# Four stationary buffers of a split-precision encoder block moved to other byte offsets in SBUF

## Chip, core and metric

The kernel runs on one core of a Trainium2 chip. The metric is the device time of one execution in microseconds (us), lower is better. One execution was also taken with the hardware profiler, and the rows below are from that one.

## What is computed

One encoder block on a sequence of 1024 tokens with 1024 features, in float32. Cut to what matters here:

```python
mod = silu(c) @ w_ada + b_ada                      # 6 rows: shift, scale, gate, twice
h = rmsnorm(x, g_norm1) * (1 + sc1) + sh1
z = h @ w_in                                       # 1024x1024 @ 1024x7168: seven groups of 1024 columns
y_a = (b_a * depthwise_conv(c_a * x_a, conv_a)) @ w_a_out
u = depthwise_conv(u_b * sigmoid(v_b), conv_b) + b_conv_b       # 31 taps
y_b = silu(layernorm(u, ln_g, ln_b)) @ w_b_out
x = x + gt1 * ((sigmoid(g_a) * y_a + sigmoid(g_b) * y_b) @ w_o)
h = rmsnorm(x, g_norm2) * (1 + sc2) + sh2
# top-1 of 4 groups, then top-2 of its 8 experts; rows sorted into blocks of 128 of one expert
yb = (silu(xblk @ w_gate[e]) * (xblk @ w_up[e])) @ w_down[e]
x = x + gt2 * scatter(w * yb)
out = rmsnorm(x, g_final)
```

## The kernel before

**Split products.** Every large matrix is kept as two float32r parts: `hi`, the value cast to float32r, and `lo`, what is left of it. The helper `three` issues three matmuls for each product of a 128x128 stationary tile and a 128x512 moving tile: hi by hi (line 1688), hi by lo (line 1689) and lo by hi (line 1690). Each matmul comes with its own weight load (LDWEIGHTS), also where two in a row have the same stationary tile. In the profile a matmul is written `ps<-moving,stationary`, so `ps<-A_hi,w_hi` has the weights `w_hi` as its stationary operand and `A_hi` as its moving one.

**Stages, in order of time.**
1. Set-up, until about 68 us: modulation rows, norm, transposes of the input.
2. The input projection: 56 slabs of weights (8 channel groups of 7 kinds), then 8 slabs of `w_a_out` and 8 of `w_b_out`, until about 840 us. A slab is 1024x128 weights. It is loaded into one of three slots of `w_raw`, ScalarE casts it to `w_hi` (line 816), VectorE writes `w_lo = w_raw - w_hi` (line 1097), and TensorE runs 48 matmuls with slices `w_hi[:, slot, k*128:(k+1)*128]` and the same of `w_lo` as stationary operand. The moving operand is `A_hi`/`A_lo`, for `w_b_out` `B_hi`/`B_lo`. Meanwhile VectorE does the two depthwise convolutions (line 1260 makes most of the 31 taps of the longer one).
3. The output projection `w_o`, until about 950 us: stationary `A_hi`/`A_lo`, moving `B_hi`/`B_lo`. Router and block tables follow until about 1000 us. The router matmul (line 1909) has the stationary operand `s2`, for the last tile `x1T_last`.
4. The experts, until about 1560 us: 33 blocks, in a loop that is unrolled four times. Each block has 48 matmuls with stationary `xT_hi`/`xT_lo` (gate and up, moving `e_hi`/`e_lo`) and 24 with stationary `hT_hi`/`hT_lo` (down). ScalarE casts each expert chunk to `e_hi` (lines 963, 969), VectorE makes `e_lo` (lines 1552, 1556). In front of these stand eight transposes of the token rows (line 2013) and, in the middle of gate and up, four of the hidden rows (line 2018).
5. The last blocks, the final norm and the stores.

All engines run the code in the order in which it is written, with semaphores between them.

**Places in SBUF.** All buffers are put by hand with `at(name, offset, ...)`, which adds a base address. `T4` is 4096 bytes. `oA`, `oAl`, `oB`, `oBl`, `oW`, `oS`, `oR` and `oM` are the offsets of regions, each before the change a multiple of 4096, and later stages use the same bytes under other names. `oX`, the expert stage's region for `xT_hi` and `xT_lo`, is a multiple of 4096 too. In this text the place of a buffer is its offset from the base modulo 512. The moving slices of the split products step by 2048 or 4096 bytes and the stationary ones by 512, so that each buffer's place is also that of each of its slices. Before the change it is 0 for every stationary and every moving buffer of `three`. Some operands of other matmuls lie elsewhere: `ident`, `ones`, `mean_w` and `s2` at 128, `same_token` at 256.

Of the kernel before, what the change touches and what calls it, by code (L numbers as in the profile page):

```python
# [26 lines left out]
F32 = mybir.dt.float32  # L27
F32R = mybir.dt.float32r
# [5 lines left out]
P = 128  # L34
# [38 lines left out]
def encoder_block(nc, x, c, w_ada, b_ada, g_norm1, w_in, conv_a, w_a_out, conv_b, b_conv_b, ln_g, ln_b,  # L73
                  w_b_out, w_o, g_norm2, w_rg, b_rg, w_re, b_re, w_gate, w_up, w_down, g_final, out):
    S, D = x.shape
    KT = D // P
# [8 lines left out]
    FT = F // P  # L85
# [7 lines left out]
    with ExitStack() as ctx:  # L93
# [3 lines left out]
        def at(name, offset, shape, dtype):  # L97
            return nc.alloc_sbuf_tensor_at(name, shape, dtype, offset=base + offset)

        T4 = 4 * D  # L100
        oA, oAl, oB, oBl = 0, 8 * T4, 16 * T4, 24 * T4
        oW = 32 * T4
        oS = oW + 9 * T4
        oR = oS + 4 * T4
        oM = oR + 4 * T4

        A_hi = at("A_hi", oA, [P, KT, S], F32R)
        A_lo = at("A_lo", oAl, [P, KT, S], F32R)
# [20 lines left out]
        conv_acc_b = at("conv_acc_b", oBl + 4 * T4 + 32, [P, S], F32)  # L129
        gate_st = at("gate_st", oBl + 5 * T4 + 32, [P, 2, S], F32)  # L130
        w_raw = at("w_raw", oW, [P, 3, KT * P], F32)
        w_hi = at("w_hi", oW + 3 * T4, [P, 3, KT * P], F32R)
        w_lo = at("w_lo", oW + 6 * T4, [P, 3, KT * P], F32R)
        wo_buf = [at(f"wo_raw{i}", oW + o * T4, [P, D], F32) for i, o in enumerate((4, 7, 5, 8))]
        stream = at("stream", oS, [P, 4, D], F32)
        rows = at("rows", oR, [P, 4, D], F32)
        GT1, SH2, A2, GT2 = range(4)
# [93 lines left out]
        s_last = at("s_last", oM + 2624, [P, 1], I32)  # L231
        act_warm = at("act_warm", oM + 2656, [P, 1], F32)
        hT_hi = at("hT_hi", oM + 4096, [P, FT, P], F32R)
        hT_lo = at("hT_lo", oM + 4096 + 2048, [P, FT, P], F32R)


        NCH = 6
# [1902 lines left out]
```

## Time and profile before

| | |
|---|---|
| time, median of 3 runs | 1593.94 us (1591.94 to 1595.24) |
| time of the profiled execution | 1591.27 us |
| its span, first to last instruction | 1589.6 us |
| TensorE (PE) busy | 1551.8 us, 98% |
| VectorE (DVE) busy | 1317.7 us, 83% |
| ScalarE (ACT) busy | 677.8 us, 43% |
| GpSimd (POOL) busy | 356.1 us, 22% |
| mean granted TensorE clock | 0.992 |

The span is shorter than the execution by 1.67 us, which lies around it. Matmuls are pipelined: the duration of one runs from its start until its result has drained, and the next one starts before that. So the rate of TensorE is read from the distance between the starts of two matmuls, which is called the pitch here, and not from their duration. PEld is the weight load, which has rows of its own.

### The profile page before, as it was taken

The numbers are of one execution on the slowest core, as the hardware profiler recorded it, in microseconds if no ns is written. First come the engines' busy times: TensorE is split into PE (matmuls) and PEld (weight loads), VectorE is DVE, ScalarE is ACT, GpSimd is POOL, SyncE is SP. The second block draws the span as 40 slices with busy tenths as digits, with TensorE's granted clock in tenths as the row PEclk, the third lists the DMA queues.
The fourth block names the chain that finished last, engine by engine and source line by source line (L and its number), as shares of the span: only waits on it lengthen the run. The fifth ranks groups of instructions, "written<-read, shape, count | busy, mean of one in ns | idle before, by whom it ended". The sixth has DMA issues, their size and how long they took to land.

```text
span 1589.6 us, 21208 instructions
## 1 busy us (share of the span) xinstructions
PE 1551.8 (98%) x7106; PEld 1272.9 (80%) x7106; DVE 1317.7 (83%) x1127; ACT 677.8 (43%) x574; POOL 356.1 (22%) x225
## 2 busy tenths in 40 slices
PE   8999999999999999999999999999999999999994
PEld 4788888888888888878888887788888888888882
DVE  5696969797978787798447469999999999999996
ACT  6511111111111010334223126777777777777764
POOL 2000000000001010000001003354455445554541
PEclk9999999999999999999999999999999999999997
DMA  9241323232323241744554347999999999999976
GB/s 358 97 120 67 119 90 108 92 117 68 119 66 119 66 124 49 238 139 133 176 174 152 119 151 292 399 371 398 398 371 376 385 379 393 376 392 392 378 274 240
DMA packets 167951, 352.61 MB, mean 222 GB/s; under 512 B 17479, under 2 KB 91239, under 8 KB 167907
## 3 DMA queue, kind: packets, MB, share of 16 engines
q1 hardware_dynamic: 150836, 309.57, 53.1%
q0 software_dynamic: 16992, 42.32, 8.8%
q8 instruction: 25, 0.41, 0.1%
q10 hardware_dynamic: 81, 0.17, 0.0%
q14 instruction: 17, 0.14, 0.0%
HBM read 324.90 MB, written 46.67 MB: 234 GB/s over the span
## 4 chain that ended last, share of the span: by engine, by line
PE 88%; DVE 5%; DMA 3%; issue 2%; ACT 1%; SPq 0%; DVEq 0%; POOLq 0%; POOL 0%; ACTq 0%
PE ps L1688 28%; PE ps L1690 28%; PE ps L1689 28%; PE ps L2013 2%; DMA xn<-in_x_dram 1%; PE ps L2018 1%; DMA w_raw<-in_w_in_dram 1%; DVE e_lo L1552 1%; PE ps L1909 1%; PE ps L1823 1%; DVE f_o L1652 0%; DVE s L1332 0%; PE ps L1893 0%; DMA e_raw<-in_w_up_dram 0%; DMA e_raw<-in_w_down_dram 0%
## 5 line engine op out<-in xcount | busy, mean ns | idle before, releaser
L1688 PE MATMUL ps<-A_hi,w_hi 128*128 128x512 f32 x1024 | 400.0, 391 | 2.3 <-DVE A_lo L1180 1.8
L1690 PE MATMUL ps<-A_hi,w_lo 128*128 128x512 f32 x1024 | 398.4, 389 | 0.0
L1689 PE MATMUL ps<-A_lo,w_hi 128*128 128x512 f32 x1024 | 398.4, 389 | 0.0
L1260 DVE SCALAR_TENSOR_TENSOR conv_acc_b<-glu,colc,conv_acc_b 128x1024 f32<-128x1024 f32 x232 | 298.0, 1285 | 10.2 <-DVE rows L1243 0.6
L1552 DVE TENSOR_TENSOR e_lo<-e_raw,e_hi 128x2048 fp32r<-128x2048 f32 x132 | 300.7, 2286 | 4.1 <-ACT e_hi L963 3.6
L963 ACT CAST e_hi<-e_raw 128x2048 fp32r<-128x2048 f32 x132 | 252.2, 1913 | 44.7 <-PE ps L1690 36.0
L1688 PEld LDWEIGHTS ps<-A_hi,w_hi 128*128 128x128 f32 x1024 | 192.2, 188 | 44.8 <-issue 3.9
L1689 PEld LDWEIGHTS ps<-A_lo,w_hi 128*128 128x128 f32 x1024 | 192.2, 188 | 40.4 <-issue 0.7
L1690 PEld LDWEIGHTS ps<-A_hi,w_lo 128*128 128x128 f32 x1024 | 192.2, 188 | 40.0
L1688 PE MATMUL ps<-e_hi,xT_hi 128*128 128x512 f32 x528 | 212.2, 402 | 0.0
L1690 PE MATMUL ps<-e_hi,xT_lo 128*128 128x512 f32 x528 | 206.4, 391 | 0.0
L1689 PE MATMUL ps<-e_lo,xT_hi 128*128 128x512 f32 x528 | 205.7, 390 | 0.0
L1556 DVE TENSOR_TENSOR e_lo<-e_raw,e_hi 128x2048 fp32r<-128x2048 f32 x64 | 146.0, 2283 | 0.0
L700 POOL DMA_INDIRECT d_x<-y_sb,s_idx x31 | 85.9, 2771 | 252.1 <-DVE y_sb L1577 228.0
L816 ACT CAST w_hi<-w_raw 128x1024 fp32r<-128x1024 f32 x72 | 73.7, 1046 | 156.5 <-PE ps L1690 153.4
L1097 DVE TENSOR_TENSOR w_lo<-w_raw,w_hi 128x1024 fp32r<-128x1024 f32 x72 | 88.0, 1223 | 60.9 <-ACT w_hi L816 57.7
L969 ACT CAST e_hi<-e_raw 128x2048 fp32r<-128x2048 f32 x64 | 122.4, 1915 | 37.5 <-PE ps L1690 37.5
L1690 PEld LDWEIGHTS ps<-e_hi,xT_lo 128*128 128x128 f32 x528 | 99.1, 188 | 21.9
L1688 PEld LDWEIGHTS ps<-e_hi,xT_hi 128*128 128x128 f32 x528 | 99.6, 189 | 18.9 <-DVE e_lo L1552 0.2
L1689 PEld LDWEIGHTS ps<-e_lo,xT_hi 128*128 128x128 f32 x528 | 99.4, 188 | 18.8
L696 POOL DMA_INDIRECT xg<-d_h,g_idx x33 | 101.2, 3067 | 28.3 <-POOL g_idx L694 28.3
L1688 PE MATMUL ps<-e_hi,hT_hi 128*128 128x512 f32 x264 | 103.0, 390 | 3.6 <-DVE hT_lo L1571 3.6
(329 smaller groups left out, 2028.5 us busy)
## 6 DMA issues: line engine op xcount, KB each, us to landing
e_raw<-in_w_gate_dram SPq DMA_DIRECT2D x132, 512.0 KB, 5.6
e_raw<-in_w_up_dram SPq DMA_DIRECT2D x132, 512.0 KB, 7.1
e_raw<-in_w_down_dram SPq DMA_DIRECT2D x66, 1024.0 KB, 7.8
w_raw<-in_w_in_dram SPq DMA_DIRECT2D x56, 512.0 KB, 4.3
stream<-in_w_ada_dram SPq DMA_DIRECT2D x36, 512.0 KB, 6.0
xn<-in_x_dram SPq DMA_DIRECT2D x8, 512.0 KB, 11.1
ada_a<-in_w_ada_dram SPq DMA_DIRECT2D x8, 512.0 KB, 10.1
d_short<-conv_acc_a POOLq DMA_DIRECT2D x8, 512.0 KB, 4.0
```

The costliest lines, as they stand in the source:

```text
L696: g.indirect_dma_start(xg[:, slot, :], None, d_h2, bass.IndirectOffsetOnAxis(ap=g_idx[:, slot:slot + 1], axis=0), bounds_check=S - 1, oob_ ...
L700: g.indirect_dma_start(d_x1, bass.IndirectOffsetOnAxis(ap=idx_ap, axis=0), rows_ap, None, bounds_check=S - 1, oob_is_err=False, compute_op ...
L816: a.copy(w_hi[:, slot, :], w_raw[:, slot, :]).then_inc(w_hi_done, 1)
L963: a.copy(e_hi[:, q, :], e_raw[:, q, :]).then_inc(gu_hi, 1)
L969: a.copy(e_hi[:, 4 + q, :], e_raw[:, 4 + q, :]).then_inc(d_hi, 1)
L1097: v.tensor_tensor(w_lo[:, slot, :], w_raw[:, slot, :], w_hi[:, slot, :].bitcast(F32), ALU.subtract).then_inc(w_lo_done, 1)
L1260: lstep(v.scalar_tensor_tensor(conv_acc_b[:], glu[:, t:t + S], w, conv_acc_b[:], ALU.mult, ALU.add))
L1552: v.tensor_tensor(e_lo[:, q, :], e_raw[:, q, :], e_hi[:, q, :].bitcast(F32), ALU.subtract).then_inc(gu_lo, 1)
L1556: v.tensor_tensor(e_lo[:, 4 + q, :], e_raw[:, 4 + q, :], e_hi[:, 4 + q, :].bitcast(F32), ALU.subtract).then_inc(d_lo, 1)
L1688: t.matmul(dst, st_hi, mv_hi, start=first, stop=False)
L1689: t.matmul(dst, st_hi, mv_lo, start=False, stop=False)
L1690: return t.matmul(dst, st_lo, mv_hi, start=False, stop=last)
```

## The change

Nothing but addresses: no instruction, operand shape, order or semaphore is touched, and the instruction lists of all five engines are the same as before, row for row.

```diff
-        oS = oW + 9 * T4
+        oS = oW + 9 * T4 + 256
         oR = oS + 4 * T4
-        oM = oR + 4 * T4
+        oM = oR + 4 * T4 + 32
...
-        w_hi = at("w_hi", oW + 3 * T4, [P, 3, KT * P], F32R)
-        w_lo = at("w_lo", oW + 6 * T4, [P, 3, KT * P], F32R)
-        wo_buf = [at(f"wo_raw{i}", oW + o * T4, [P, D], F32) for i, o in enumerate((4, 7, 5, 8))]
+        w_hi = at("w_hi", oW + 3 * T4 + 64, [P, 3, KT * P], F32R)
+        w_lo = at("w_lo", oW + 6 * T4 + 256, [P, 3, KT * P], F32R)
+        wo_buf = [at(f"wo_raw{i}", oW + o * T4 + shift, [P, D], F32) for i, (o, shift) in enumerate(((4, 64), (7, 256), (5, 64), (8, 256)))]
...
-        hT_lo = at("hT_lo", oM + 4096 + 2048, [P, FT, P], F32R)
+        hT_lo = at("hT_lo", oM + 4096 + 2176, [P, FT, P], F32R)
```

`w_hi` goes to place 64, `w_lo` to 256, `hT_hi` to 288 and `hT_lo` to 416. The stationary buffers `A_hi`, `A_lo`, `xT_hi` and `xT_lo` stay at 0, as do all moving operands of `three`. With `oS`, `stream` and `rows` move by 256 bytes. With `oM`, everything behind it moves by 288: `glu`, `s2`, `ident`, `ones`, `mean_w`, the small columns and the tables of the expert stage. `wo_buf`, four buffers for raw rows of `w_o`, lies in slots of `w_hi` and `w_lo` and goes with them. All moves are multiples of 32 bytes.

## Rows read from the trace of the kernel before

**Rows 1.** The profile page: busy share, and the granted clock in 40 slices

```profile
PE 1551.8 (98%) x7106; PEld 1272.9 (80%) x7106; DVE 1317.7 (83%) x1127; ACT 677.8 (43%) x574; POOL 356.1 (22%) x225
...
PEclk9999999999999999999999999999999999999997
```

**Rows 2.** The page's chain that ended last, by engine

```profile
PE 88%; DVE 5%; DMA 3%; issue 2%; ACT 1%; SPq 0%; DVEq 0%; POOLq 0%; POOL 0%; ACTq 0%
```

**Rows 3.** Windows (from:to, length, busy us and count): projections, experts, one block

```profile
68.00:840.00 772.00, 771.68 (x3382) 634.27 (x3382) 602.25 (x482) 152.74 (x153) 36.53 (x40) 1.00 0.36 114
...
1000.00:1550.00 550.00, 550.00 (x2593) 459.15 (x2593) 542.49 (x341) 409.02 (x275) 277.62 (x125) 1.00 1.00 377
...
1100.80:1118.60 17.80, 17.80 (x86) 14.87 (x85) 17.77 (x12) 13.37 (x9) 9.19 (x5) 1.00 1.03 404
```

**Rows 4.** Groups by line and form on PE: count, busy us, mean ns

```profile
L1688 PE MATMUL ps<-A_hi,w_hi 128*128 128x512 f32 x1024 | 400.0, 391 | 2.3 <-DVE A_lo L1180 1.8 <-DVE A_lo L1189 0.3 <-DVE w_lo L1097 0.2
...
L1688 PE MATMUL ps<-e_hi,xT_hi 128*128 128x512 f32 x528 | 212.2, 402 | 0.0
...
L1688 PE MATMUL ps<-e_hi,hT_hi 128*128 128x512 f32 x264 | 103.0, 390 | 3.6 <-DVE hT_lo L1571 3.6
...
L1688 PE MATMUL ps<-B_hi,A_hi 128*128 128x512 f32 x128 | 50.3, 393 | 0.0
L1688 PE MATMUL ps<-B_hi,w_hi 128*128 128x512 f32 x128 | 50.0, 391 | 0.3 <-DVE w_lo L1097 0.3
```

**Rows 5.** Timeline (start us, us) in the projection: nineteenth after first, and one pair

```profile
726.71 0.39 PE L1688 MATMUL ps<-A_hi,w_hi 128*128 128x512 f32 x1
...
730.79 0.39 PE L1688 MATMUL ps<-A_hi,w_hi 128*128 128x512 f32 x1
...
300.17 0.39 PE L1688 MATMUL ps<-A_hi,w_hi 128*128 128x512 f32 x1
300.17 0.19 PEld L1689 LDWEIGHTS ps<-A_lo,w_hi 128*128 128x128 f32 x1
```

**Rows 6.** Timeline of PE just behind the four transposes of a block

```profile
1101.43 0.40 PE L1689 MATMUL ps<-e_lo,xT_hi 128*128 128x512 f32 x1
...
1101.90 0.40 PE L1688 MATMUL ps<-e_hi,xT_hi 128*128 128x512 f32 x1
...
1103.75 0.39 PE L1690 MATMUL ps<-e_hi,xT_lo 128*128 128x512 f32 x1
```

**Rows 7.** Timeline of PE, matmuls of plain float32 and the router's

```profile
18.81 0.59 PE L1719 MATMUL ps<-ada_a,diag_c 128*128 128x512 f32 x1
...
20.12 1.88 PE L1719 MATMUL ps<-ada_a,diag_c 128*128 128x512 f32 x4
...
679.65 1.88 PE L1817 MATMUL ps<-conf_sum,mean_w 128*128 128x512 f32 x4
...
873.66 1.40 PE L1909 MATMUL ps<-w_r,s 128*128 128x36 f32 x11
...
947.80 1.40 PE L1909 MATMUL ps<-w_r,x1T_last 128*128 128x36 f32 x11
...
1566.18 1.88 PE L2110 MATMUL ps<-y_prev,same_token 128*128 128x512 f32 x4
```

**Rows 8.** One line's durations: the taps on DVE, min/median/max ns

```profile
L1260 DVE SCALAR_TENSOR_TENSOR conv_acc_b<-glu,colc,conv_acc_b x232: 1277/1285/1290, 71.4 to 684.0; 128x1024 f32<-128x1024 f32 x116
```

**Rows 9.** The page's groups of the two that write the weight parts

```profile
L816 ACT CAST w_hi<-w_raw 128x1024 fp32r<-128x1024 f32 x72 | 73.7, 1046 | 156.5 <-PE ps L1690 153.4
L1097 DVE TENSOR_TENSOR w_lo<-w_raw,w_hi 128x1024 fp32r<-128x1024 f32 x72 | 88.0, 1223 | 60.9 <-ACT w_hi L816 57.7
```

**Rows 10.** The page's DMA issues: the only large loads whose target moves

```profile
stream<-in_w_ada_dram SPq DMA_DIRECT2D x36, 512.0 KB, 6.0
```

## Prediction

> **What bounds the kernel.** I read the page first: TensorE is busy 98% of the span, at the full granted clock until the last slice [rows 1], and the chain that ended last runs over TensorE for 88% of it [rows 2]. The windows by stage say the same of each stage: 771.68 of 772 us in the two projections, where VectorE has 602, and 550 of 550 us among the experts, where VectorE has 542.5 and the DMA engines are busy all the time [rows 3]. The groups show that TensorE hardly waits: 2.3 us before all first matmuls of the projection, 3.6 us before those of the down product [rows 4]. So a change that moves no instruction can do something only if it changes what one matmul costs, and then almost every nanosecond counts.
>
> What one costs is the pitch. From the first to the nineteenth start of the projection rows are 4.08 us for 18 matmuls, 226.7 ns each, and the load of the next weights starts together with each matmul [rows 5]. The reader is to see that the duration of 389 to 391 ns [rows 4] is no cost; the pitch is.
>
> **The change part by part.** It removes, adds and orders nothing. Three kinds of operand move.
>
> *Stationary reads of TensorE.* With `w_hi` and `w_lo` as stationary operand there are three times 1024 matmuls of A and three times 128 of B, 3456 in all; with `hT_hi` and `hT_lo` three times 264, which is 792 [rows 4]. Together 4248. One nanosecond of pitch is 3.46 us in the projections and 0.79 us among the experts. The price per matmul is not shown by the trace, since all operands of `three` lie at place 0, so I bound it.
>
> From above in time: directly behind the transposes the same instructions, with the same places, run slower. The first two steps take 0.47 us, 235 ns each, and the first ten 2.32 us, 232 ns each, before the pitch falls to its steady value [rows 6]. So the pitch isn't a constant of the instruction: how weight load and moving stream fall against each other has a price of 5.3 ns (mean) to 8.3 ns (worst). If a new place held them in such a relation for good, that would be 4248 x 5.3 = 22.5 us to 4248 x 8.3 = 35.3 us.
>
> From below: a plain float32 matmul of 512 columns has a pitch of (1.88 - 0.59) / 3 = 430 ns, and a weight load of its own each time [rows 7]. If it streams its columns twice, one stream takes 215 ns beside a weight load, an estimate from these rows. The split matmul streams once and takes 226.7. The 11.7 ns between may be what the weight load takes from the moving stream when that runs at full rate. If another place took all of it away, the projections would win 3456 x 11.7 = 40.4 us. Among the experts it would be 792 x 11.7 = 9.3 us, but VectorE leaves no more than 550 - 542.5 = 7.5 us there [rows 3]. The lower bound is therefore -47.9 us.
>
> Which value between? I take 0, for three reasons from rows. First, where stationary operands at different places can be compared they cost the same: `diag_c` at 0, `mean_w` at 128 and `same_token` at 256 all give 1.88 us for four, and the router's weight loads from `s2` at 128 and from `x1T_last` at 0 both give 1.40 us for eleven, at most 127 ns each, though their moving operand has 36 columns and the load of 128 columns is the longer part [rows 7]. A weight load by itself doesn't care where it reads. Second, a load reads one run of exactly 512 bytes, and a moving stream beside it reads four such runs. [...] Third, 226.7 ns holds for operands that lie far apart in different ways (A with w, B with w, B with A, e with hT, means of 389 to 393 ns in all of them [rows 4]). None of this tests a full-rate stream at another place, so the chance stays well under certainty.
>
> [...]
>
> *VectorE and ScalarE.* VectorE writes `w_lo` 72 times and reads `w_hi`, `rows`, `stream`, `glu` and `hT_hi` at new places. The 232 taps of line 1260 read `glu` from starts that lie 4 bytes apart, and all take 1277 to 1290 ns [rows 8]. So place costs VectorE at most those 13 ns, and for the 72 + 31 + 33 instructions on `w_lo`, `y_sb` and `hT_lo` that is 1.8 us of engine time. The part in the projections lies under TensorE, since VectorE has 170 us to spare there [rows 3]; without that cover the 72 would cost 0.9 us. The cast to `w_hi` has 153 us of waiting for TensorE ahead of it [rows 9]. In the expert block VectorE is busy 17.77 of 17.80 us [rows 3], so the rest, 64 x 13 ns = 0.8 us, is the most that could show. I take 0.
>
> *DMA.* `w_raw` and the expert chunks don't move. Only `stream`'s target does, by 256 bytes, in 512 KB loads that take 6.0 us [rows 10] in a stage where the DMA engines are 36% busy [rows 3]. I take 0. If a load took 10% longer it would land 0.6 us later, and what it feeds would have to be waited for to show.
>
> **Sum.** 1591.27 + 0 + 0 + 0 = 1591.3 us for a profiled execution. That one lay 2.7 us under the median of the runs shown, so for the median I add it again: 1593.9 us. What a measurement of this kernel can tell from no change is about 0.2%, 3.2 us here, or 0.75 ns on each of the 4248 matmuls. A dependence on place that is there at all would most likely be larger than that, so the cases stand apart.
>
> **The rivals.**
> 1. *The place frees the moving stream.* For it: the 11.7 ns that no wait explains, equal places of weights and moving operand, and the fact that they start in the same instant [rows 5], so that they begin on the same spot of every 512 bytes. Against it: the three reasons above. At full effect 1593.9 - 40.4 = 1553.5 us, with what VectorE lets through among the experts down to 1546.0. Since the four buffers have four places, a part is as likely as the whole: with half the effect, or with only `w_hi` helped in part, 1574. [...]
> 2. *The place fixes a worse relation.* One mechanism: each matmul keeps the pitch that now lasts only ten matmuls behind a transposition [rows 6], because load and stream no longer start on the same spot. It is decided by whether 226.7 ns is the settled best or merely the value for place 0. Price 22.5 us, 1616.4 us in all; with only one of the stationary pair affected about half, 1605; at worst 1629.2. It turns from no change to slower at 0.75 ns per matmul. Among the experts nothing absorbs it, as TensorE has no idle time there. Against it: the pitch always falls back to 226.7 by itself, and does so in all pairings.
> 3. *The places cancel.* `w_hi` serves two of three matmuls and `w_lo` one. A gain on one and a loss on the other would end near zero with both pitches changed. It is counted in the forecast's chance, and a small part of it in the others.
>
> **How the numbers follow.** No change within 0.2%: 0.56. Rival 1: 0.24, since the unexplained 11.7 ns needs some cause. Rival 2: 0.20. The likeliest case's own range is 1590.7 to 1597.1 us. To hold 8 in 10 the range must take in 0.24 of the others. I put half of rival 1 at a gain of 24 us or less, which reaches to 1570, and rather more than half of rival 2 at a loss of 12 us or less, to 1606. What stays outside is 0.12 and 0.08.
>
> **What would show it.** In the profile of the changed kernel, the pitch of `ps<-A_hi,w_hi` to `ps<-A_lo,w_hi` and of `ps<-A_hi,w_lo` should be 227 ns as before; `ps<-e_hi,xT_hi` and `ps<-B_hi,A_hi`, whose stationary buffers stay, are the control in any case. The projection window should still hold some 3382 matmuls in 772 us, and the expert block 17.80 us. Rival 1 would show a pitch toward 215 ns on `w_hi` or `w_lo` rows alone and a projection stage of 732 us, while the block would shrink by a few tenths at most. Rival 2 would show 230 to 235 ns in both. A different stage length at an unchanged pitch would mean that I missed a wait, and a block longer than 17.80 us at an unchanged pitch would put it on VectorE. The prediction is wrong if a full-rate moving stream and a weight load do disturb each other by where they lie, which nothing in the trace of before could try.

## The result and the profile after

The changed kernel takes 1614.85 us (median of 4 runs, 1610.91 to 1617.51) against 1592.94 us for the kernel before on the same occasions: a ratio of 1.0137, 95% interval 1.0123 to 1.0152. It is slower by about 22 us, outside the range of 1570 to 1606, and close to the 1616.4 us of rival 2.

The page of the changed kernel, its busy row and its chain, show a longer span and no new wait of TensorE:

```profile
PE 1580.3 (98%) x7106; PEld 1274.5 (79%) x7106; DVE 1317.8 (82%) x1127; ACT 677.0 (42%) x574; POOL 305.3 (19%) x225
...
PE 91%; DVE 3%; DMA 3%; issue 1%; ACT 0%; SPq 0%; DVEq 0%; POOLq 0%; POOL 0%; ACTq 0%
```

Against [rows 1] VectorE has the same 1317.8 us of work, ScalarE too, and TensorE 28.5 us more. The windows of the same stretches as in [rows 3] show where it is:

```profile
68.00:840.00 772.00, 772.00 (x3293) 617.05 (x3292) 588.33 (x470) 144.30 (x144) 36.52 (x40) 1.00 0.34 108
1000.00:1550.00 550.00, 547.47 (x2571) 453.86 (x2570) 541.83 (x340) 411.80 (x279) 224.05 (x122) 1.00 1.02 383
1124.00:1141.90 17.90, 17.90 (x85) 14.87 (x84) 17.70 (x13) 13.37 (x9) 9.29 (x6) 1.00 1.03 403
```

In the same 772 us TensorE is as busy and gets through 3293 matmuls, not 3382. The granted clock of that window is 1.00 in both kernels, and 0.992 in the mean of both executions, so it is not the clock. (The 547.47 busy us in the window from 1000 us are no new wait: everything there stands 22 us later, so that the window now takes in the first waits of the expert stage. From 1022.3 us on TensorE is busy for 527.68 of 527.70 us.) The groups by form (count, busy us, mean ns) say which ones take longer:

```profile
L1688 PE MATMUL ps<-A_hi,w_hi 128*128 128x512 f32 x1024 | 405.9, 396 | 0.3 <-DVE A_lo L1189 0.3
...
L1688 PE MATMUL ps<-e_hi,xT_hi 128*128 128x512 f32 x528 | 211.2, 400 | 0.0
...
L1688 PE MATMUL ps<-e_hi,hT_hi 128*128 128x512 f32 x264 | 104.9, 397 | 3.3 <-DVE hT_lo L1571 3.3
```

A mean of 396 for `w_hi` stands against 391 in [rows 4] and 397 for `hT_hi` against 390, while `xT_hi`, whose place stayed, has 400 and 402. The timeline gives the pitch. These are the first and the eighth `A_hi,w_hi` of a stretch. Each of them is followed by its `A_lo,w_hi` and `A_hi,w_lo`, so the two rows are 21 matmuls apart:

```profile
299.63 0.40 PE L1688 MATMUL ps<-A_hi,w_hi 128*128 128x512 f32 x1
...
304.52 0.39 PE L1688 MATMUL ps<-A_hi,w_hi 128*128 128x512 f32 x1
```

4.89 us for 21 is 233 ns, against 226.7 in [rows 5]. The sum closes. With A as moving operand the 3072 matmuls run from 43.6 to 751.2 us before and from 45.0 to 772.1 us after (starts of `A_hi,w_hi`), 707.6 and 727.0 us, which is 19.4 us or 6.3 ns each. With B it is 753.0 to 839.8 before and 773.2 to 862.3 after (starts of `B_hi,w_lo`), 2.3 us more. The down products lie between 999.8 and 1563.8 us before and 1022.3 and 1590.1 us after (starts of `e_hi,hT_hi`), 3.8 us more; the distance from block to block grew from 17.80 to 17.92 us. Together 25.5 us, where the two spans differ by 26.3 us. The first projection also began 1.4 us later in this execution, and 0.7 us came back between the last `A_hi,w_hi` and the first `B_hi,w_lo` (1.8 us before, 1.1 after). This execution was the slowest of the four of the changed kernel; the medians differ by 21.9 us.

### The profile page after: what moved, and what is told of

Same layout as the page of the kernel before. It is cut to its first block, busy times and chain, and to the rows that moved or that the text cites. A ratio compares the mean times of both kernels' runs of the same rounds, so it can differ in the third digit from the quotient of the medians.

```text
span 1615.9 us, 21208 instructions
## 1 busy us (share of the span) xinstructions
PE 1580.3 (98%) x7106; PEld 1274.5 (79%) x7106; DVE 1317.8 (82%) x1127; ACT 677.0 (42%) x574; POOL 305.3 (19%) x225
## 4 chain that ended last, share of the span: by engine, by line
PE 91%; DVE 3%; DMA 3%; issue 1%; ACT 0%; SPq 0%; DVEq 0%; POOLq 0%; POOL 0%; ACTq 0%
PE ps L1690 29%; PE ps L1688 29%; PE ps L1689 29%; PE ps L2013 2%; DMA xn<-in_x_dram 1%; PE ps L2018 1%; DMA stream<-in_w_ada_dram 1%; PE ps L1909 1%; DVE e_lo L1552 1%; PE ps L1823 1%; DVE f_o L1652 0%; PE ps L1893 0%; DVE e_lo L1556 0%; DMA e_raw<-in_w_down_dram 0%; PE ps L1817 0%
## 5 line engine op out<-in xcount | busy, mean ns | idle before, releaser
L1688 PE MATMUL ps<-A_hi,w_hi 128*128 128x512 f32 x1024 | 405.9, 396 | 0.3 <-DVE A_lo L1189 0.3
L1690 PE MATMUL ps<-A_hi,w_lo 128*128 128x512 f32 x1024 | 405.3, 396 | 0.0
L1689 PE MATMUL ps<-A_lo,w_hi 128*128 128x512 f32 x1024 | 403.3, 394 | 0.0
L1689 PE MATMUL ps<-e_lo,hT_hi 128*128 128x512 f32 x264 | 103.8, 393 | 0.0
## 6 DMA issues: line engine op xcount, KB each, us to landing
xn<-in_x_dram SPq DMA_DIRECT2D x8, 512.0 KB, 11.1
```

The costliest lines, as they stand in the source:

```text
L1688: t.matmul(dst, st_hi, mv_hi, start=first, stop=False)
L1689: t.matmul(dst, st_hi, mv_lo, start=False, stop=False)
L1690: return t.matmul(dst, st_lo, mv_hi, start=False, stop=last)
```

## Experiments

### 1. The pattern by itself, at 28 combinations of places

A kernel with nothing but the split matmuls. `hi` and `lo` are the places of the stationary pair, `m` is that of the moving operand. The code is shortened, and the line of the moving slices is put in words (in bytes); the slices of `st` are in elements of 4 bytes:

```python
for r in range(2):
    for k in range(8):
        for h in range(2):
            m_hi, m_lo = moving slices at (k % 4) * 4096 + h * 2048 + m, two buffers
            s_hi, s_lo = st[:, hi + k * P:hi + (k + 1) * P], st[:, lo + k * P:lo + (k + 1) * P]
            t.matmul(dst, s_hi, m_hi, start=k == 0, stop=False)
            t.matmul(dst, s_hi, m_lo, start=False, stop=False)
            t.matmul(dst, s_lo, m_hi, start=False, stop=k == 7)
```

> This kernel leaves the block's computation out: it runs nothing but the split matmul pattern (hi by hi, hi by lo, lo by hi, 128x512, a weight load each) 96 times in each of 28 sections, with eight plain float32 matmuls between sections. Section by section the places of the stationary pair and of the moving operand differ: 16 sections with hi and lo at the same place 0, 32, ... 480 and the moving operand at 0; six with unequal pairs, those of the change among them; six with the moving operand at 64 or 256 too, and two places below 32 bytes. Theory A, the distance between stationary and moving place sets the pitch: it goes up and down over the 16 sections by some ns around 227, 64/64/64 and 256/256/256 have the 226.7 ns of 0/0/0. Theory B, the stationary buffer's own place does: 64/64/64 is as slow as 64/64/0. Theory C, only an unequal pair is slow, because each load finds another relation than the one before: all 16 equal sections have 226.7 ns and 64/256/0 and 288/416/0 have 231 to 234 ns.

Like all sweeps here, this is one profiled execution. The steady pitch, worked out from the starts of the matmuls behind the 24th of each section:

| place of hi and lo, moving operand at 0 | ns |
|---|---|
| 0 and 256 | 226.7, 226.7 |
| 32 and 288 | 233.3, 233.3 |
| 64 and 320 | 233.2, 233.2 |
| 96 and 352 | 234.3, 234.3 |
| 128 and 384 | 232.3, 232.3 |
| 160 and 416 | 233.3, 233.3 |
| 192 and 448 | 228.9, 228.9 |
| 224 and 480 | 233.3, 233.3 |

Places 256 apart are one place. Of the other sections, 4 and 16 have 232.4 and 233.3 ns, the pair (0, 64) has 231.1, (64, 0) has 233.3, and (0, 256), (256, 0) and place 0 with the moving operand at 256 have 226.7. The same can be read straight from the timeline, at the starts of the plain matmuls that stand between sections. The distance of two such rows is one section of 96 split matmuls with the plain ones next to it:

```profile
173.29 0.49 PE L67 MATMUL ps<-raw 128*128 128x128 f32 x3
197.06 0.49 PE L67 MATMUL ps<-raw 128*128 128x128 f32 x3
221.25 0.49 PE L67 MATMUL ps<-raw 128*128 128x128 f32 x3
244.84 0.49 PE L67 MATMUL ps<-raw 128*128 128x128 f32 x3
...
556.96 0.49 PE L67 MATMUL ps<-raw 128*128 128x128 f32 x3
580.54 0.49 PE L67 MATMUL ps<-raw 128*128 128x128 f32 x3
604.12 0.49 PE L67 MATMUL ps<-raw 128*128 128x128 f32 x3
627.90 0.49 PE L67 MATMUL ps<-raw 128*128 128x128 f32 x3
```

The first four enclose the sections 192, 224 and 256: 23.77, 24.19 and 23.59 us. The last four enclose 64 and 256 with the moving operand at the same place, both 23.58 us, as fast as 0, and then stationary 0 with the moving operand at 64: 23.78 us, which is the value of 192, that is of -64. So theory A holds: what counts is the distance from the moving operand, modulo 256 bytes. B falls. C falls too, since equal pairs are slow at seven of eight places. The pairs of the change gave 231.1 ns, both (64, 256) and (288, 416).

### 2. The parts of the change, and the distance, in the kernel

Diffs of kernels are against the changed kernel, unless the text says otherwise. They are cut to the buffers that matter; `wo_buf` goes with the slots that it lies in each time. First, only hT and the small buffers stay moved:

```diff
-        w_hi = at("w_hi", oW + 3 * T4 + 64, [P, 3, KT * P], F32R)
-        w_lo = at("w_lo", oW + 6 * T4 + 256, [P, 3, KT * P], F32R)
+        w_hi = at("w_hi", oW + 3 * T4, [P, 3, KT * P], F32R)
+        w_lo = at("w_lo", oW + 6 * T4, [P, 3, KT * P], F32R)
```

> The changed kernel with w_hi, w_lo and the raw rows of w_o back at place 0, so that only hT_hi (288) and hT_lo (416) and the small buffers stay moved. If the loss is the sum of 3456 matmuls with w and 792 with hT at some 6 ns each, the projections are back at their old length and the time is 1594 + 4 = 1598 us, with an expert block of 17.92 us. If the loss came from a moved small buffer or from stream and rows, it stays near 1615 us.

1595.51 us, ratio 1.0022 (1.0011 to 1.0034), a block distance of 17.92 us and 226.7 ns with w. The ratio stands for 3.5 us, the medians differ by 2.6. In the profile the down products span 3.9 us more than before and the projections are back to within 1 us. So that is the experts' part, and the small buffers, `stream` and `rows` cost nothing that can be seen.

Both of a pair at one place:

```diff
-        w_lo = at("w_lo", oW + 6 * T4 + 256, [P, 3, KT * P], F32R)
+        w_lo = at("w_lo", oW + 6 * T4 + 64, [P, 3, KT * P], F32R)
...
-        hT_lo = at("hT_lo", oM + 4096 + 2176, [P, FT, P], F32R)
+        hT_lo = at("hT_lo", oM + 4096 + 2048, [P, FT, P], F32R)
```

> The changed kernel with hi and lo of each pair at one place: w_hi and w_lo at 64, hT_hi and hT_lo at 288. Theory C (only unequal pairs are slow) gives the time of before, 1593 us. Theories A and B (the place itself) give 233 ns on the matmuls with w if 64 is a bad place, 1610 to 1617 us, or anything down to 1593 us if it is 256 that is bad.

1619.23 us, ratio 1.0170 (1.0153 to 1.0186), slower than the change itself, with a block of 17.97 us. Its timeline, 21 matmuls from the first row to the second:

```profile
299.85 0.39 PE L1688 MATMUL ps<-A_hi,w_hi 128*128 128x512 f32 x1
...
304.75 0.39 PE L1688 MATMUL ps<-A_hi,w_hi 128*128 128x512 f32 x1
```

4.90 us, 233.3 ns. Theory C falls in the kernel too.

Everything moved together, as a diff against the kernel before:

```diff
-        base = (nc.sbuf_base + 63) // 64 * 64
+        base = (nc.sbuf_base + 63) // 64 * 64 + 64
```

> The kernel of before with the base of all buffers 64 bytes later, so that all distances between buffers stay. Theory A (distance) gives the time of before, 1593 us within 3 us, and 226.7 ns. Theory B (the buffer's own place) gives another pitch on all 6216 split matmuls; at the 233 ns that the changed kernel shows this is up to 6216 x 6.3 = 39 us more.

1591.83 us, ratio 1.0003 (0.9990 to 1.0015), 226.7 ns with w and a block of 17.80 us. All addresses changed and all distances stayed: the time is that of before.

### 3. Which of the two, and the rule of 256 bytes

The first sweep makes a statement on the diff: `w_lo` at 256 is the same as at 0, so that `w_hi` alone does the harm in the projections. Three kernels test this and the rule. First w moved as in the change, with hT at a distance of 256:

```diff
-        hT_hi = at("hT_hi", oM + 4096, [P, FT, P], F32R)
-        hT_lo = at("hT_lo", oM + 4096 + 2176, [P, FT, P], F32R)
+        hT_hi = at("hT_hi", oM + 4064, [P, FT, P], F32R)
+        hT_lo = at("hT_lo", oM + 4064 + 2048, [P, FT, P], F32R)
```

> The changed kernel with hT_hi and hT_lo at a distance of 256 from the moving operand, which the first sweep found as good as 0; w_hi and w_lo stay at 64 and 256. By the sweep the loss of 26 us in the profile splits into 4 of the experts, which go, and 22 of the projections, which stay: 1611 us, expert block 17.80 us. If an expert block of 17.92 us stays, the rule of 256 bytes does not hold in the kernel.

1612.85 us, ratio 1.0128 (1.0109 to 1.0147), block distance 17.81 us. The split is as expected. In its profile the pitch with w was another one, though, with the same places of w as in the change:

```profile
299.81 0.39 PE L1688 MATMUL ps<-A_hi,w_hi 128*128 128x512 f32 x1
...
304.66 0.39 PE L1688 MATMUL ps<-A_hi,w_hi 128*128 128x512 f32 x1
```

4.85 us for 21, 231 ns (231.1 over whole slabs). The changed kernel's profile has 233.3 ns up to the 59th slab, and changes in the middle of that one:

```profile
705.49 0.40 PE L1688 MATMUL ps<-A_hi,w_hi 128*128 128x512 f32 x1
...
707.59 0.40 PE L1688 MATMUL ps<-A_hi,w_hi 128*128 128x512 f32 x1
...
708.29 1.88 PE L1817 MATMUL ps<-conf,mean_w 128*128 128x512 f32 x4
...
712.79 0.39 PE L1688 MATMUL ps<-A_hi,w_hi 128*128 128x512 f32 x1
...
714.87 0.39 PE L1688 MATMUL ps<-A_hi,w_hi 128*128 128x512 f32 x1
```

Nine matmuls take 2.10 us ahead of the `conf,mean_w` and 2.08 us behind them, 233.3 and 231.1 ns. The pitch stays at 231.1 until the transposition `ident,mrow` at 795.03 us, two slabs into `w_b_out`, and is 233.3 behind that. The kernel of this section has 231.1 from its first slab, 233.3 for the 24 matmuls between a `rows,ones` and the `conf,mean_w` of the 59th slab, 231.1 behind them and again 233.3 behind `ident,mrow`. So one pair of places can settle at more than one pitch, and in both profiles every change lies right behind matmuls of another kind; what chose another value for the first slab is not shown. Over 3456 matmuls the two values are 8 us apart. That can be why the runs of the changed kernel spread over 6.6 us, but single runs without a profile don't show it.

All four at a distance of 256:

```diff
-        w_hi = at("w_hi", oW + 3 * T4 + 64, [P, 3, KT * P], F32R)
+        w_hi = at("w_hi", oW + 3 * T4 + 256, [P, 3, KT * P], F32R)
```

(and `hT_hi`, `hT_lo` as in the diff above)

> The changed kernel with w_hi, w_lo, hT_hi and hT_lo all 256 bytes past the moving operand's place, everything else as in the changed kernel. The sweep's rule (distance modulo 256) gives the time of before, 1593 us, a pitch of 226.7 ns and 17.80 us per block. Any distance other than 0 modulo 512 being bad gives 1610 us or more.

1593.76 us, ratio 1.0004 (0.9993 to 1.0015), block distance 17.81 us, 226.7 ns with w. The rule of 256 bytes holds.

Only `w_hi` put back:

```diff
-        w_hi = at("w_hi", oW + 3 * T4 + 64, [P, 3, KT * P], F32R)
+        w_hi = at("w_hi", oW + 3 * T4, [P, 3, KT * P], F32R)
```

> The changed kernel with only w_hi (and the raw rows of w_o in its slots) back at place 0; w_lo stays at 256, hT_hi at 288, hT_lo at 416. The sweep holds 256 to be the same as 0, so that w_hi's 64 bytes carry the whole loss of the projections: 1597 us, an expert block of 17.92 us, the pitch with w back to 226.7. If the 256 bytes of w_lo had a part in it, a third of the 22 us or more would stay, 1604 us.

```profile
299.82 0.39 PE L1688 MATMUL ps<-A_hi,w_hi 128*128 128x512 f32 x1
...
304.58 0.39 PE L1688 MATMUL ps<-A_hi,w_hi 128*128 128x512 f32 x1
```

4.76 us for 21, 226.7 ns, and 1595.81 us, ratio 1.0018 (1.0007 to 1.0029). One offset of 64 bytes in one buffer carries the loss of the projections. The 3 us that remain are those of hT: the blocks are 17.92 us apart and the down products span 3.8 us more than before.

### 4. Is there a better place than 0?

> The block's computation is left out again: 64 sections of 48 split matmuls, hi and lo at the same place, from 0 to 252 bytes in steps of 4, the moving operand at 0. The first sweep gave one and the same pitch for places 256 apart: 226.7 ns at 0, 228.8 at 192, 232.3 to 234.3 elsewhere. Theory A1, what counts is only whether the distance is 0: all others in between have 228 to 235 ns and none is under 226.7. Theory A2, the distance works through a finer pattern that steps of 32 bytes missed: some place, near 0 or near 192 most likely, is under 226.7 ns, down to 215 ns, and would beat both kernels.

Every place from 0 to 252 in steps of 4, hi and lo alike, a section of 48 matmuls each. 226.67 ns at 0, 120, 132 and 240; 230.0 at 12, 24, 44, 60, 100 and 108; 228.9 at 192; the others lie between 230.0 and 237.5, most often at 233.3, and 156 has 243.3. Between neighbours there is no slope: 120 has 226.7, and 116 and 124 have 233.3 and 231.7. The starts of the plain matmuls around the sections 116, 120 and 124, 48 matmuls each:

```profile
404.48 0.49 PE L67 MATMUL ps<-raw 128*128 128x128 f32 x3
417.47 0.49 PE L67 MATMUL ps<-raw 128*128 128x128 f32 x3
430.18 0.49 PE L67 MATMUL ps<-raw 128*128 128x128 f32 x3
443.08 0.49 PE L67 MATMUL ps<-raw 128*128 128x128 f32 x3
```

12.99, 12.71 and 12.90 us. None of the 64 is under 226.67.

Unequal pairs out of 0, 16, 64, 100, 120, 132, 192 and 240:

> Computation left out: 56 sections of 48 split matmuls with the stationary hi and lo at unequal places out of 0, 16, 64, 100, 120, 132, 192 and 240, the moving operands at 0. If each matmul pays for its own load's distance, a mixed pair costs the mean of the two equal ones, weighted two to one for hi: (0, 64) 228.9 ns, (64, 0) 231.1, (120, 240) 226.7. The first sweep's (0, 64) with 231.0 and (64, 0) with 233.3 speak for the rival: the pair as a whole settles into a pattern of its own, and no mean of parts gives it. No pair is expected under 226.7 ns; one that is would be a way to a faster kernel.

Of 56 pairs 20 have 226.67 ns and none has less; the others reach 235.6. Parts don't add up: (100, 0) has 226.7 and (0, 100) 232.6, and (120, 16) has 226.7 though (16, 16) has 233.3. The mean of the parts, which one theory expected, is off by more than 7 ns, at (192, 120) and (192, 132); a pair settles as a whole, as the rival said.

The sweep's oddest claim is that 120 bytes are as good as 0. It was tried in the kernel, where each buffer is taken as a slice that begins 24 bytes into one at 96:

```diff
-        w_hi = at("w_hi", oW + 3 * T4 + 64, [P, 3, KT * P], F32R)
+        w_hi = at("w_hi", oW + 3 * T4 + 96, [P, 3 * KT * P + 8], F32R)[:, 6:6 + 3 * KT * P].rearrange("p (s n) -> p s n", s=3)
```

(`w_lo`, the raw rows of `w_o`, `hT_hi` and `hT_lo` likewise)

> w_hi, w_lo, hT_hi and hT_lo all 120 bytes (modulo 256) past the moving operand, a place that the fine sweep found as good as 0, between neighbours of 233 and 232 ns. If the sweep describes the kernel: 1593 us, 226.7 ns with w. If only equal places are good in the kernel and the sweep's 120 was an accident of its starting state, 1610 to 1620 us.

```profile
300.11 0.39 PE L1688 MATMUL ps<-A_hi,w_hi 128*128 128x512 f32 x1
...
304.87 0.39 PE L1688 MATMUL ps<-A_hi,w_hi 128*128 128x512 f32 x1
```

4.76 us for 21, 226.7 ns, and 1592.51 us, ratio 0.9998 (0.9987 to 1.0009). 120 bytes off is as good as 0, where the change costs 22 us. The kernel of before stands at the best pitch that these runs found.

### 5. What the excess depends on

> Computation left out: the same pattern at place 0 and at 64, with weights of 128, 96, 64 and 32 columns under a stream of 512, with streams of 256 and 384 columns, and with both operands read as plain float32. If the weight load takes its reads out of the moving stream, the pitch above 512 columns' own time falls with the columns of the weights: at place 0 from 226.7 by some 2.7 ns for each 32 columns less, at place 64 from 233 by some 4.5 ns, and the excess stays the same for shorter streams (120 and 126 ns at 256 columns). If the excess belongs to a float32r matmul as such, it doesn't change with the weights' columns. Plain float32 streams at half the rate: 429 ns at both places.

| columns of weights, stream of 512 | place 0, ns | place 64, ns |
|---|---|---|
| 128 | 226.7 | 233.4 |
| 96 | 230.0 | 228.4 |
| 64 | 229.9 | 232.7 |
| 32 | 231.6 | 231.1 |

The pitch does not fall with the weights' columns, so the expected 2.7 to 4.5 ns for each 32 columns are not there: the excess does not go with the number of columns that the load reads. Which place is better even turns round at 96, and at 32. In plain float32 both places have 429.2 ns from row to row. Each plain float32 matmul of the program leaves two rows there, 192 for 96, each with a weight load, so that one matmul takes 858.3 ns. The float32r matmuls of this run at place 0 have 120.0, 173.3 and 226.7 ns for 256, 384 and 512 columns, 53.3 ns for each 128 columns more and so 213.3 ns for 512. A plain float32 row takes 2.5 ns more than twice that, and these two places cost the same, so the first of my three reasons compared operands where I can find no price for place.

The simplest form, one stationary and one moving slice over and over:

> Computation left out: 48 matmuls of one stationary slice and one moving slice per section, ten places of the stationary slice, with 512 and 256 columns of stream; then ten sections in which the moving slice alternates between two places. [...] If what counts is how one stream ends and the next one begins, the excess differs between the lengths and follows the moving slice's own steps, also where the stationary slice stays: (0, 480 step) unlike (0, 512 step).

Whole sections of 48 in the timeline (start us, length us). In order: place 0, place 64 and place 120 with 512 columns; 0 and 64 with 256; 0 and 64 with 496:

```profile
34.05 11.15 PE L74 MATMUL ps<-mv,sa 128*128 128x512 f32 x48
...
72.69 11.45 PE L74 MATMUL ps<-mv,sb 128*128 128x512 f32 x48
...
98.70 11.13 PE L74 MATMUL ps<-mv,sb 128*128 128x512 f32 x48
...
162.81 5.99 PE L74 MATMUL ps<-mv,sa 128*128 128x256 f32 x48
...
185.28 5.90 PE L74 MATMUL ps<-mv,sb 128*128 128x256 f32 x48
...
249.65 10.97 PE L74 MATMUL ps<-mv,sb 128*128 128x496 f32 x48
...
295.94 11.12 PE L74 MATMUL ps<-mv,sb 128*128 128x496 f32 x48
```

The settled pitches are 226.7, 233.3 and 226.7 ns; 120.0 and 117.8; 223.3 and 226.7. Neither the split pattern nor any other engine is needed for the effect, since from 30 to 360 us only one instruction of 1.01 us ran on another engine. At 256 columns the order is reversed: place 0 is the slowest of ten (120.0), the others have 117.4 to 119.6. So "equal places are best" holds for a stream of 512 columns and not in general. At place 0 the pitch is 120.0, 173.3 and 226.7 ns for 256, 384 and 512 columns: each 128 columns more cost 53.3 ns, and 13.3 ns are left over in all three when the columns are taken off at that slope. This rest is called the excess here. At place 64 the pitches are 117.8, 176.7 and 233.3 ns, an excess of 11.1, 16.7 and 20.0 ns. With 480 and 448 columns place 0 has 216.7 and 202.7 ns, an excess of 16.7 and 16.0 ns. At 240 bytes this pattern has 228.3 ns at 512 columns, where the split pattern had 226.7: a place found in one pattern need not hold for another. The theory of how one stream ends and the next begins holds in part only: at place 64 the excess differs between the lengths, at place 0 it is the same for 256, 384 and 512 columns. Letting the moving slice alternate by 64 bytes at place 0 gave 230.8 ns, against 226.7 with the slice at rest.

## Why the prediction was wrong

- *What bounds the kernel.* Right. TensorE set the end before and after, a change of pitch went through to the end almost in full, and the weight was right: 6.3 ns on 3072 matmuls gave 19.4 us.
- *VectorE, ScalarE, DMA at 0.* Right. With hT moved alone, and all small buffers with it, the projections had their old pitch and the total was 3.5 us up, which the down products explain.
- *The price of a stationary place.* This is the step that failed: "Which value between? I take 0". In its place the runs show 6.3 ns in the mean on the matmuls with w and 4.5 ns on those with hT (231.7 against 227.2, the mean pitch of the down products in the two profiles). The three reasons each failed in their own way. The first compared plain float32 matmuls and bare weight loads, and for plain float32 the sweep shows no price at place 64 either (429.2 ns a row at both). It also took place 256 for another place than 0, and for the split matmuls it is the same one (226.7 ns at both). The second set the 512 bytes of a load beside the four such runs of a stream. These sizes are the same at every place, and yet pitches settle at 226.7, 228.9, 230.0, 231.1 or 233.3 ns and jump between neighbours 4 bytes apart (233.3, 226.7 and 231.7 at 116, 120 and 124 bytes). Which reads of load and stream meet, and what that costs, no run shows. The third compared buffers that all lay at distance 0, which is what made them equal.
- *The upper bound.* Right in kind, and close in size partly by luck. The rows behind the transposes [rows 6] gave 5.3 ns in the mean and 8.3 ns at worst; the steady price of the changed places was 6.3 ns in the projections. 22.5 us stood in rival 2, and 22 us came. The 5.3 ns are the mean of a stretch that is settling, though, and the real terms were others: 6.3 ns on w, 4.5 ns on hT, 25.5 us in the profiled execution. That the 5.3 to 8.3 ns come from how load and stream fall against each other was my reading, and no run shows it. What the first sweep's single distances show is that a slow pitch can last. Behind the plain matmuls, place 0 runs through 230, 231, 236, 228, 233, 231 and then stays at 227 ns, while place 64 goes on between 231 and 236. That stretch was the evidence: the same instructions at another pitch. I read it and then gave the case 0.20.
- *The lower bound.* Too low. Of the 11.7 ns, an estimate from half the 430 ns of a plain float32 row, none was to be had at 512 columns, in 64 equal places and 62 unequal pairs: the lowest settled pitch is 226.7 ns. That such a row streams its columns twice was part of the estimate and is not shown.
- *Rival 2's mechanism.* Its deciding question was whether 226.7 ns is the settled best or the value of place 0. It is the best found. "No longer start on the same spot" was too narrow: 120, 132 and 240 bytes off are as good.
- *Rival 3, the places cancel.* Wrong: `w_lo` at 256 has no price (226.7 ns with only `w_hi` put back), so there was nothing to cancel.

Still open is what in the chip makes the price. The runs show that it is there for float32r and, at places 0 and 64, not for plain float32. It depends on the distance of stationary and moving operand modulo 256 bytes and on the length of the stream, and can settle at two values for the same places (231.1 and 233.3 ns). No run had matmuls without a weight load each, or another data type, so that the load's part in it is not shown. They rule out the absolute address (as far as 64 and 256 bytes were tried), other engines and a cost in proportion to the weights' columns.

## What to carry to other kernels

These rows are for weights of 128 columns in float32r with a load for each matmul. Where such a product is bound by TensorE, measure the pitch of its matmuls from start to start, and treat the distance between the stationary and the moving buffer, modulo 256 bytes, as a tuning parameter: on 512 columns most places cost 3% of the pitch here (233.3 against 226.7 ns). Keep stationary slices at distance 0 (a step of 256 or 512 bytes keeps that), and measure again if the moving operand has another width, since at 256 columns distance 0 was the slowest of ten. When a trace shows one instruction at several pitches, as here 232 ns over ten matmuls and 226.7 ns behind them, something that isn't in its operands has a price, and "no row shows another value" is no reason for 0.

## What the runs showed of the hardware that I had not expected

- One SBUF buffer, `w_hi`, 64 bytes from where it was cost 6.3 ns in the mean per 128x512 float32r matmul of the projections, 19.4 us over the 3072 with A, in a kernel of 1593 us.
- The dependence has a period of 256 bytes: eight places and the eight 256 bytes further on agree to 0.1 ns, at 512 columns.
- It is jagged: 226.7 ns at 120 bytes, 233.3 at 116, 231.7 at 124.
- The same places can settle at 233.3 or 231.1 ns, and the value changed only behind matmuls of another kind.
- At place 0 the pitch is 53.3 ns for each 128 columns and 13.3 ns besides (120.0, 173.3 and 226.7 ns at 256, 384 and 512 columns). A row of plain float32 with 512 columns has 429.2 ns, 2.5 ns above twice the 213.3 ns that this slope gives for 512 columns, and a matmul leaves two of them.
